# Strassen's scheme in six of the eleven gate and up column groups of five feed-forward layers on one Trainium2 core

## What is computed

```python
# D_MODEL = 1024, D_FF = 2816, SEQ = 256, float32
def swiglu(x, w_gu, w_down):                     # w_gu: 1024 x 5632, w_down: 2816 x 1024
    gate, up = jnp.split(x @ w_gu, 2, axis=-1)
    return (jax.nn.silu(gate) * up) @ w_down

# first block, once:     h = h + swiglu(rmsnorm(h, g_ffn), w_gate_up, w_down)
# second block, 4 times: h = h + 0.5 * rmsnorm_2(swiglu(rmsnorm_2(h, g), w_gu, w_down), g2)
```

## Time and profile before

| | before |
|---|---|
| time, median of 3 runs | 1316.94 us (1316.62 to 1317.17) |
| span of the profiled execution, first to last instruction | 1315.4 us |
| instructions | 16971, of them 6137 matmuls and transposes on PE |
| busy: PE, PEld, DVE, ACT, POOL | 99%, 82%, 58%, 49%, 7% |
| bytes moved | 236 MB, mean 179 GB/s |

### The profile page before, as it was taken

How to read it: one execution, slowest core, us unless ns; L and a number is a source line. 1 busy time by engine, 2 the same in 40 slices (tenths; PEclk the granted TensorE clock), 3 DMA queues, 4 the chain that set the end, 5 groups by cost and what they waited for, 6 DMA issues and landing times.

```text
span 1315.4 us, 16971 instructions
## 1 busy us (share of the span) xinstructions
PE 1304.2 (99%) x6137; PEld 1074.4 (82%) x6137; DVE 761.6 (58%) x877; ACT 650.5 (49%) x898; POOL 91.3 (7%) x146
## 2 busy tenths in 40 slices
PE   9999999999999999999999999999999999999998
PEld 7888888888888888788888887888888877788886
DVE  6776664445555545766745546754456568745554
ACT  6675654443554444645644444644445566644443
POOL 6141000000000000100100000100001001100000
PEclk9999999999999999999999999999999999999999
DMA  9534465555465555565555555555556534655551
GB/s 327 169 98 160 129 202 184 185 185 188 160 212 184 186 186 190 180 198 168 195 188 191 191 191 193 170 184 185 186 188 197 178 119 129 205 184 183 186 190 58
DMA packets 163484, 236.02 MB, mean 179 GB/s; under 512 B 7744, under 2 KB 120568, under 8 KB 163440
## 3 DMA queue, kind: packets, MB, share of 16 engines
q1 hardware_dynamic: 161152, 229.67, 53.6%
q0 software_dynamic: 1840, 4.64, 1.2%
q10 hardware_dynamic: 448, 1.12, 0.2%
HBM read 234.35 MB, written 1.05 MB: 179 GB/s over the span
## 4 chain that ended last, share of the span: by engine, by line
PE 96%; DVE 2%; ACT 1%; issue 1%; POOL 0%; DVEq 0%; ACTq 0%
PE B L1674 22%; PE B L1676 22%; PE B L1675 22%; PE B L2113 8%; PE B L2115 8%; PE B L2114 8%; PE T L2126 2%; PE T L1668 1%; PE B L2285 0%; DVE w_lo L1053 0%; PE B L1668 0%; PE B L1810 0%; PE T L1795 0%; PE B L1831 0%; DVE w_lo L1204 0%
## 5 line engine op out<-in xcount | busy, mean ns | idle before, releaser
L1053 DVE TENSOR_TENSOR w_lo<-w_raw,w_hi 128x2048 fp32r<-128x2048 f32 x209 | 480.1, 2298 | 280.3 <-ACT w_hi L557 280.2
L557 ACT ACTIVATE w_hi<-w_raw 128x2048 fp32r<-128x2048 f32 x209 | 399.9, 1915 | 152.5 <-PE B L2115 120.8
L1674 PE MATMUL B<-w_hi,xt_lo 128*128 128x512 f32 x1152 | 459.2, 399 | 3.5 <-DVE xt_lo L1068 0.9
L1676 PE MATMUL B<-w_hi,xt_hi 128*128 128x512 f32 x1152 | 449.7, 390 | 0.0
L1675 PE MATMUL B<-w_lo,xt_hi 128*128 128x512 f32 x1152 | 448.6, 389 | 0.0
L1674 PEld LDWEIGHTS B<-w_hi,xt_lo 128*128 128x128 f32 x1152 | 216.4, 188 | 51.0 <-issue 6.2
L1676 PEld LDWEIGHTS B<-w_hi,xt_hi 128*128 128x128 f32 x1152 | 216.1, 188 | 46.6
L1675 PEld LDWEIGHTS B<-w_lo,xt_hi 128*128 128x128 f32 x1152 | 216.6, 188 | 41.5
L2113 PE MATMUL B<-w_hi,act_lo 128*128 128x512 f32 x400 | 156.3, 391 | 0.0
L2115 PE MATMUL B<-w_hi,act_hi 128*128 128x512 f32 x400 | 155.7, 389 | 0.0
L2114 PE MATMUL B<-w_lo,act_hi 128*128 128x512 f32 x400 | 155.6, 389 | 0.0
(11 more groups left out here) (279 smaller groups left out, 977.8 us busy)
## 6 DMA issues: line engine op xcount, KB each, us to landing
w_raw<-in_ffn_w_gu SPq DMA_DIRECT2D x176, 512.0 KB, 4.7
w_raw<-in_ffn_w_down SPq DMA_DIRECT2D x88, 512.0 KB, 4.0
w_raw<-in_w_gate_up SPq DMA_DIRECT2D x44, 512.0 KB, 4.8
w_raw<-in_conv_w_in SPq DMA_DIRECT2D x24, 512.0 KB, 4.6
w_raw<-in_w_down SPq DMA_DIRECT2D x22, 512.0 KB, 3.9
w_raw<-in_w_in SPq DMA_DIRECT2D x16, 512.0 KB, 7.4
w_raw<-in_w_kv SPq DMA_DIRECT2D x16, 512.0 KB, 4.8
w_raw<-in_w_mem_kv SPq DMA_DIRECT2D x8, 512.0 KB, 4.4
```

Of the source, the lines that this page charges most:

```text
L557: act.activation(whi[slot if to is None else to][:, :], raw[slot][:, :], ACT.Copy).then_inc(w_hi, 1)
L1053: dve.tensor_tensor(wlo[o][:, :], raw[slot][:, :], whi[o][:, :].bitcast(F32), ALU.subtract)\
L1674: pe.matmul(bank[:, :], lo[:, k, x], whi[s][:, c], start=first, stop=False)
L1676: return pe.matmul(bank[:, :], hi[:, k, x], whi[s][:, c], start=False, stop=last)
```

## The change

Per layer the groups are now: group 0 and 1 plain, then three times a pair of groups (512 gate and 512 up columns) followed by one plain group. A pair is a product of a 2x2 block matrix A (128 tokens by 512 of k; A11, A12 for the first 128 tokens) and B (512 of k by 512 columns; B11 and B21 gate, B12 and B22 up). It is computed by Strassen's scheme in Winograd's form with seven products of 12 matmuls:

- sums on x, once a layer (`x_sums`): S1 to S4 on DVE from x high + x low, one add over 128x2048 and four over 128x512, put behind the split of the first unit of group 1; their high part by ACT and low part by DVE into the `mem_T` tiles
- sums on weights, four a pair (`weight_sum`, 128x2048 adds on DVE): T1 = B11+B12, T2 = T1+B22, T3 = B12+B22, T4 = T2+B21 (the minus signs lie in the x sums and results); for the first pair of layers 1 and 3 the first three are done at the end of the layer before
- the blocks B11 to B22 are loaded by SP into `Z`, `QT` and `nat`, which are free in a feed-forward layer (`block_in`), not into `raw`
- each of P1 to P7 has a weight unit of its own that ACT and DVE split, from a block or a sum
- products accumulate in banks XB (T1), YB (B4) and ZB (B5); ACT copies P1, P5 and P6 out (`keep`), DVE makes three results of 128x512 (`result`), ACT and DVE gate both groups at once (`pair_gate`, `pair_act`)
- PE's order in a pair, by unit, is P1, Da, P5, P6, Db, P3, P7, Dn, P2, P4, Na, Nb (no Db in the first pair); Da, Db, Dn are down units of earlier groups, Na, Nb the plain group; activations of the second group of a pair have tiles of their own
- the loops are written out; units per layer go from 33 to 42, of which 33 are loaded as before
- `dist` shares a tile with `foxmask` and is loaded later, `grow1` and `grow2` lie in `VD`; the k,v rounds of L3 all stand at the end.

The core of the diff:

```diff
+PAIRS = 3
+STEP0 = ("P1", "Da", "P5", "P6", "P3", "P7", "Dn", "P2", "P4", "Na", "Nb")
+STEP = ("P1", "Da", "P5", "P6", "Db", "P3", "P7", "Dn", "P2", "P4", "Na", "Nb")
...
+        OPERAND = {"P1": "B11", "P2": "B21", "P3": "B22", "P4": "T4", "P5": "T1", "P6": "T2", "P7": "T3"}
...
 # SP, in ffn
+                up("N0a", 0)
+                if f == 2:
+                    for w in first_blocks:
+                        sp.wait_ge(*w)
+                    first_block("B11")
+                    first_block("B12")
+                up("N0b", 0)
...
+                for p in range(PAIRS):
+                    if p:
+                        up("Na", p)
+                        up("Nb", p)
+                    next_block("B22", "P3", p)
+                    next_block("B12", "P7", p)
+                    down("Da", p + 1)
+                    next_block("B21", "P2", p)
+                    next_block("B11", "P4", p)
+                    down("Db", p + 1)
+                    down("Dn", p + 1)
...
 # ACT, in ffn
+                for p in range(PAIRS):
+                    if p:
+                        block("P1", p)
+                        weights("Da", p)
+                        act_out(3 * p - 1)
+                        act_out(3 * p)
+                    block("P5", p)
+                    gate_of(1 + 2 * p, u0 + (OP["Nb", p - 1] if p else OP["N1b", 0]), GU)
+                    block("P6", p)
+                    keep("P1", p, q1, XB[:, :].rearrange("p (a c) -> p a c", a=2))
...
+                    weights("Na", p)
+                    weights("Nb", p)
+                    pair_gate(p)
...
 # DVE
+            def x_sums(name, f):
+                dve.wait_ge(xt_lo, XT[name] + TOKS * KD)
+                link(dve.tensor_tensor(xsum, xhi[:, :, :].bitcast(F32), xlo[:, :, :].bitcast(F32), ALU.add))
...
+                link(dve.tensor_tensor(a22, a21, a22, ALU.subtract))
+                dve.tensor_tensor(a21, a11, a21, ALU.subtract)
+                link(dve.tensor_tensor(a11, a22, a11, ALU.subtract))
+                dve.tensor_tensor(a12, a12, a11, ALU.add).then_inc(sx_ok, 1)
...
+                x_sums(reader, f)
+                weights("N1b", 0)
                 dve.wait_ge(rstd, 2 * ST[stat] + 2)
                 act_of(0, PAIR[0] if f else F0)
...
+                block("P1", 0)
+                if f % 2 == 0:
+                    weight_sum(1, PAIRS * f)
+                weights("Da", 0)
+                act_out(0)
+                if f % 2 == 0:
+                    weight_sum(2, PAIRS * f)
+                dve.wait_ge(sx_hi, f + 1)
+                dve.tensor_tensor(ylo[:, :, :], xsum, yhi[:, :, :].bitcast(F32), ALU.subtract).then_inc(sx_lo, 1)
+                for p in range(PAIRS):
+                    if p:
+                        block("P1", p)
+                        sums(2, p)
+                        weights("Da", p)
+                        act_out(3 * p - 1)
+                        act_out(3 * p)
+                        sums(3, p)
+                    act_of(1 + 2 * p, GU)
+                    block("P5", p)
+                    block("P6", p)
+                    if p:
+                        sums(4, p)
+                        weights("Db", p)
+                    else:
+                        if f % 2 == 0:
+                            sums(3, p)
+                        block("P3", p)
+                    act_out(3 * p + 1)
+                    if p:
+                        block("P3", p)
+                    else:
+                        sums(4, p)
+                    block("P7", p)
+                    weights("Dn", p)
+                    result(0, p)
+                    block("P2", p)
+                    result(1, p)
+                    block("P4", p)
+                    weights("Na", p)
+                    result(2, p)
+                    weights("Nb", p)
+                    pair_act(p)
+                    sums(1, p + 1)
...
+                act_out(3 * PAIRS + 1)
...
+                sums(2, PAIRS)
+                split_at(u0 + FFN_UNITS)
...
+                sums(3, PAIRS)
+                split_at(u0 + FFN_UNITS + 1)
...
 # PE, in ffn
+                up_unit("N1a", 0)
+                turn_act(0, 0)
+                up_unit("N1b", 0)
+                for p in range(PAIRS):
+                    m = 3 * (PAIRS * f + p)
+                    if p:
+                        pe.wait_ge(act_lo, FJ * f + 3 * p + 1)
+                    block("P1", p)
+                    down("Da", p)
+                    turn_act(3 * p + 1, 1 + 2 * p)
+                    if p == 0:
+                        pe.wait_ge(sx_lo, f + 1)
+                    block("P5", p)
+                    pe.wait_ge(snap, m + 1)
+                    block("P6", p)
+                    if p:
+                        down("Db", p)
+                    pe.wait_ge(snap, m + 2)
+                    block("P3", p)
+                    pe.wait_ge(snap, m + 3)
+                    block("P7", p)
+                    down("Dn", p)
+                    block("P2", p)
+                    pe.wait_ge(c_ok, m + 2)
+                    block("P4", p)
+                    pe.wait_ge(c_ok, m + 3)
+                    up_unit("Na", p)
+                    turn_act(3 * p + 2, 2 + 2 * p)
+                    turn_act(3 * p + 3, 2 + 2 * p, 256)
+                    up_unit("Nb", p)
```

More of the change, by code:

```diff
@@ L335, in ffn, with block_in @@
+            def block_in(name, p, w_gu):
                 gu = w_gu.rearrange("(k p) f -> p k f", p=P)
[L337 to L357, removed]
+                k0, col = 4 * (name[1] == "2"), 512 + 768 * p + FF * (name[2] == "2")
@@ L850, in ffn, with keep, act_out @@
+                def keep(name, p, dst, bank):
+                    act.wait_ge(w_used, u0 + OP[name, p] + 1)
+                    act.activation(dst, bank, ACT.Copy).then_inc(snap, 1)
+                def act_out(d):
+                    act.wait_ge(act_t, FJ * f + d + 1)
+                    act.activation(act_parts(d)[0][:, :], (XB if d and d % 3 == 0 else T[0])[:, :], ACT.Copy)\
+                        .then_inc(act_hi, 1)
+                weights("N1b", 0)
                 act.wait_ge(rstd, 2 * ST[stat] + 2)
@@ L2102, in up_unit, with block, down_part @@
                         for t in range(TOKS):
-                            ins = product(GU[t], slot, columns(k), k, t, k == 0, k == KD - 1)
+                            ins = product(GU[t], home(u), columns(k), k, t, k == 0, k == KD - 1)
                     ins.then_inc(w_used, 1)
-                def down(slot, t, half, first=False, last=False):
-                    hi, lo = (last_hi, last_lo) if last else (ahi, alo)
+                def block(name, p):
+                    u = u0 + OP[name, p]
+                    bank, k0, t, sums = {
+                        "P1": (XB, 0, 0, False), "P5": (ZB, 4, 1, True), "P6": (XB, 0, 0, True), "P3": (ZB, 4, 0, True),
+                        "P7": (XB, 0, 1, True), "P2": (YB, 4, 0, False), "P4": (XB, 4, 1, False)}[name]
+                    first = name in ("P1", "P5", "P2")
+                    hi, lo = (yhi, ylo) if sums else (xhi, xlo)
+                    pe.wait_ge(w_lo, u - 1)
+                    for k in range(k0, k0 + 4):
+                        ins = product(bank, home(u), columns(k), k, t, first and k == k0, k == k0 + 3, hi, lo,
+                                      not first)
+                    ins.then_inc(w_used, 1)
+                def down_part(d, u, t, half):
+                    hi, lo = act_parts(d)
+                    slot = home(u)
                     for k in range(2):
@@ L2177, in ffn @@
                         turn(nxt, 0, j, h, h_waits(nxt))
-                down(last % RING, 1, 1, last=True).then_inc(w_used, 1)
+                down_part(d, u, 1, 1).then_inc(w_used, 1)
             ffn(0, "ffn0", h_waits("ffn0"), nxt="ffn1")
```

405 lines of the change are left out of this document (259 added, 146 removed).

## The result

| | before | after |
|---|---|---|
| time, median | 1317.06 us (1316.62 to 1317.29) | 1325.1 us (1324.95 to 1327.58) |
| ratio to before, 95% interval | | 1.0066 (1.0052 to 1.0080) |
| span of the profiled execution | 1315.4 us | 1325.8 us (its time: 1327.58 us) |
| mean granted clock of PE | 0.999 | 0.996 |

A forecast was written before the change was run, and what follows sets the result against it. The prediction took PE's matmul count as the bound: 52.8 us of new waits against 40.8 us removed gave +12.0 us, so a 1327.4 us span and a 1329 us median; range 1310 to 1341 us.

The forecast's parts named there:

- Removed: On PE, 12 matmuls fewer per pair, 180 in all at 0.2267 us each: 40.8 us saved.
- The price of a weight sum: On DVE, a 128x2048 add taken at a low part's 2.21 us; lower bound half of that, upper 2.4.
- rival (a): Weight-sum adds on DVE are cheaper than a low part, so the kernel is faster, placed at 1310 us; chance 0.20.
- Wait 1: Between pairs, P1 waits for act_lo behind DVE's queue: 1.9 us, two places per layer, 18.8 us in all.
- Wait 2: At each layer's start, sums on x delay DVE and PE waits 2.6 us, 2.0 in layer 0: 12.4 us.
- Wait 3: First pair without Db: PE waits at P7, 1.15 us in layers 1 and 3, 3.83 in the others: 13.8 us.
- Wait 4: Ends of layers 0 and 2: weight sums ahead of the update of h make PE wait, 4.8 us together.
- Smaller ones: Block loads delaying N0b entering layer 2, about 2 us, and k,v transposes at layer 3's end, about 1 us.
- The clock: PE's granted clock: 2.4 us of idling at the span's end cost nothing; a fall in the new waits was given 0.06.
- (b): Gain and waits cancel at 1317 us: waits a third smaller because a few operations overlap more; chance 0.10.
- (c): Loads late: at 4.2 us per unit, B11 misses the first weight sum, waits are 65 us, time 1341; chance 0.07.
- (d): PE's clock falls in the waits at layer starts, next units at half rate: 27 us more, 1356 us; chance 0.06.

The follow-up runs named there:

- tiny sums: The changed kernel with its weight sums done on one column in place of 2048, except for the first pair of layer 0: 1299.89 us.
- the one sum moved: The changed kernel with the second weight sum of the later pairs put behind the two act_lo pieces, no work removed: 1312.2 us.
- spread kernel: The changed kernel with the same work reordered: x sums, weight sums and layer 2's block loads moved to other places in their queues: 1292.86 us.

## Why the prediction was right, and where not

The direction, the range (1310 to 1341) and the likeliest case held: 1325.1 us against 1329, +8.0 us where +12.0 was worked out. The mechanism held: the matmuls come off in full, DVE's queue makes PE wait at the places named, and the waits are worth more. The steps are less good than their sum: two errors of opposite sign cancel in part, and that the time came within 4 us is partly luck.

- **Removed, 40.8 us.** Right: 0.2268 us a matmul by the run with 200 fewer, and the count fell by 180.
- **The price of a weight sum**, the largest unknown: 2.29 us and a pitch of 2.20, the low part's, as chosen. The lower bound and rival (a) fall with it.
- **Wait 1** (18.8 us): in the right place, ten times, but 14.7 us. 1.9 us each was 0.45 too much: about half because small operations behind others have a pitch of 0.60 (I took 0.66) and the two products 1.32 (1.40), half because the hand-over from DVE to PE takes 0.06 us (236.71 to 236.77) and I put 0.25.
- **Wait 2** (12.4): 11.0. The sums on x take 4.98 us (5.1), the hand-over again 0.05. The walk was right to 0.3 us a layer.
- **Wait 3** (13.8): 11.7, the same two terms. In L0, L2 and L4 it falls into two waits, 1.04 to 1.06 us before P3 and 2.15 to 2.19 before P7, not one of 3.83; in L1 and L3 it is 1.0 us before P7 (1.15).
- **Wait 4** (4.8): 2.9. PE's transposes ask for the first piece of h only; I had counted both updates, and the longer hand-over.
- **Smaller ones** (3): 3.0, of which 2.4 at the entry of L2. PE's wait there is ACT's wait for the load of N0b less 1.90 us: 2.21 and 4.11 in after, 2.81 and 4.71 with tiny sums, 3.27 and 5.17 with the one sum moved, 3.38 and 5.28 with the sums on x moved, 1.18 and 3.08, 1.14 and 3.04 in the two of these kernels with small matmuls and a full clock. So the load's landing sets it; why the load lands up to 2.2 us later in one execution than in another stays open. With the block loads behind it, in the spread kernel, PE doesn't wait there.
- **The clock**: the step that failed. From the earlier trace rows I argued that 2.4 us without work cost nothing, so waits of about that length would not either, and gave a fall 0.06, as an all-or-nothing case of 27 us. Three of them happened, at 1.5 us each, and with them the prediction's own sign of being wrong, that the granted clock leaves 1.00 in a feed-forward layer. The row it rested on was one wait at the end of the kernel, and one wait that passes isn't a bound: in after the wait that ends at 372.77 (2.18 us idle) left the clock alone, and the one that ends at 846.80 (2.17 us) did not. The other ground, that the bursts of work are 50 us long, fails too. In front of the eight waits of about 2 us in after, PE had worked for 3 to 22 us without one of 0.25 us or more. In the kernel with tiny sums it had worked so for 156 us, and one wait of 2.16 us at the start of L1 brought half clock all the same (the rows stand below). It should have been a term of a few us in the sum.
- **The restart** behind each wait, some 2.7 us for 27 of them, was not in the sum at all, though the earlier trace rows hold its like.

The wait at the start of L1 in the kernel with tiny sums, in PE's timeline, and the stretch behind it:

```profile
367.86 0.78 PE L2404 MATMUL T<-ident,work 128*128 128x128 f32 x4 [2.16 <-DVE work L1607]
```

```profile
368.40:371.60 3.20, 3.20 (x10) 2.52 (x9) 3.20 (x2) 1.54 (x2) 0.00 (x0) 0.50 0.98 299
```

In short: waits over by 9.5 us, clock and restart short by 7.3, which makes 9.8 us of the 12.0 worked out.

Of the rivals, (b), "the waits are smaller, because operations overlap more", was right in kind, with a fifth and not a third. (c), late loads, shows only at the entry of L2. (d) came true in small. What the forecast didn't weigh is the order itself. It priced each wait to a few tenths, and most of that was the price of a place in DVE's queue, not of the work: spread out, the same work costs 14 us of new waits, and the change gives 24 us.

The Trainium skill, "TensorE: Matmul & The Clock Gate", section "HAM oscillation — how this bites in real kernels", tells of matmul bursts of some 2 us with waits of 3 to 5 us, after each of which the clock is low again. The trace agrees that a wait can bring the clock down and that the work behind pays it. It differs in size, and the measurement decides: in after waits of 2.0 to 2.2 us of idle time were followed by half clock, three of eight of that length, and in front of two of the three PE had worked for 18 and 22 us without a wait, in the kernel with tiny sums for 156.

## What to carry to other kernels

When PE is the bound and helpers have room on average, trading matmuls for helper work pays by the place in the helper's queue: walk the queue, and put every added operation behind the pieces that PE asks for next. Here that decided between 8 us lost and 24 us won. Where several added operations stand in one stretch, moving one moves the wait to the next unit; spread them over all stretches with slack. When new waits of about 2 us are left on PE, count a fall of the clock for some of them, and try small matmuls inside the wait, ahead of what PE waits for and never behind it.

## What the runs showed of the hardware

- Waits of 2.0 to 3.4 us of idle time on PE brought the granted clock from 1.00 to 0.50 in some places and executions and not in others of the same length: a wait of 2.00 us did (sums on x moved, L2), one of 2.87 us didn't (spread kernel, L4). In the profiled executions of all kernels the 18 falls before the end of the program stand at such waits, and none at a shorter one. The times of one kernel spread over 8 us (1308.1 to 1316.3), and over 0.6 us once the waits held small matmuls.
- At 1.2 GHz a matmul of 512 columns starts every 0.43 us, at 2.4 GHz every 0.227; each fall cost 1.5 to 1.6 us where full work followed and 0.1 us where a wait did.
- Adding 64 matmuls of 128x128 to PE made the kernel 3.6 us faster in one order and 7.1 in another.
- A DVE sum of two fp32 tiles of 128x2048 with fp32 output takes 2.29 us, as does the same with fp32r output; on 128x1 it takes 0.15.
